# Two paddings in the SBUF layout: the activation pairs of a two-layer encoder and decoder begin 64 bytes behind a multiple of 128

## The reference

```python
for l in range(2):                                   # encoder
    h = h + 0.5 * swiglu_ffn(rms_norm(h), ffn1_w_in[l], ffn1_w_out[l])     # 1024 -> 2 x 2816 -> 1024
    h = h + hybrid_mixer(rms_norm(h), ...)           # stick-breaking heads and gated-delta heads, in and out projection
    h = h + memory_cross_attention(rms_norm(h), rms_norm(mem), ...)
    h = h + 0.5 * swiglu_ffn(rms_norm(h), ffn2_w_in[l], ffn2_w_out[l])
x = rms_norm(h)
for l in range(2):                                   # decoder
    x = hybrid_layer(x, ...)                         # three kinds of attention, gates, up and out projections
```

## Time and profile before

| | |
|---|---|
| median of 3 runs | 1866.68 us |
| the profiled execution's own time | 1862.87 us |
| its span, first to last instruction | 1861.1 us |
| TensorE busy, matmuls | 1832.1 us, 98% |
| VectorE busy | 1221.3 us, 66% |
| ScalarE busy | 961.9 us, 52% |
| DMA engines, mean | 48.5% of 16 engines' span, 162 GB/s |
| granted TensorE clock | 1.00 of full speed throughout |

### The profile page before, as it was taken

One profiled execution on the slowest core, in us unless ns is written; L12 is line 12 of the kernel. 1 busy time (PEld: TensorE's weight loads), 2 busy tenths in 40 slices (PEclk: granted clock), 3 DMA queues, 4 the chain that ended last, 5 costly groups with the idle time before them and its releaser, 6 DMA issues.

```text
span 1861.1 us, 35544 instructions
## 1 busy us (share of the span) xinstructions
PE 1832.1 (98%) x15226; PEld 1736.5 (93%) x15226; DVE 1221.3 (66%) x1876; ACT 961.9 (52%) x1475; POOL 67.9 (4%) x32
## 2 busy tenths in 40 slices
PE   7999999999999999999999999999999999999999
PEld 7999998899999999999988999999988989988889
DVE  6775576765766567756767657665774678763676
ACT  6544467364544455444673545444653565553562
POOL 0000011400000000000114000000000000000000
PEclk9999999999999999999999999999999999999999
DMA  8565543333555655555433335555446435446332
GB/s 330 194 193 183 173 145 114 103 126 124 182 189 185 205 186 188 183 187 174 148 113 102 127 114 181 187 187 182 159 158 205 136 104 179 160 147 215 125 114 91
DMA packets 84460, 302.39 MB, mean 162 GB/s; under 512 B 9168, under 2 KB 11728, under 8 KB 84176
## 3 DMA queue, kind: packets, MB, share of 16 engines
q1 hardware_dynamic: 84304, 300.13, 48.5%
HBM read 299.04 MB, written 1.05 MB: 161 GB/s over the span
## 4 chain that ended last, share of the span: by engine, by line
PE 92%; DVE 5%; ACT 2%; issue 1%; DMA 0%; SPq 0%; DVEq 0%; ACTq 0%
PE bank L395 23%; PE bank L398 22%; PE bank L399 22%; PE bank L701 2%; PE bank L930 1%; DVE w_lo L1564 1%; PE bank L417 1%; PE bank L416 1%; PE bank L413 1%; PE bank L628 1%; PE bank L1015 1%; PE bank L460 1%; PE bank L1066 1%; PE bank L464 1%; PE bank L465 1%; PE bank L903 1%
## 5 line engine op out<-in xcount | busy, mean ns | idle before, releaser
L1564 DVE TENSOR_TENSOR w_lo<-ring,w_hi 128x1024 fp32r<-128x1024 f32 x544 | 660.0, 1248 | 112.2 <-ACT w_hi L1133 111.5
L1133 ACT ACTIVATE w_hi<-ring 128x1024 fp32r<-128x1024 f32 x544 | 564.5, 1055 | 276.9 <-PE bank L395 220.8
L395 PE MATMUL bank<-xs,w_hi 128*128 128x256 f32 x2448 | 691.6, 283 | 0.0
L399 PE MATMUL bank<-xs,w_lo 128*128 128x256 f32 x2448 | 682.1, 279 | 0.0
L398 PE MATMUL bank<-xs,w_hi 128*128 128x256 f32 x2448 | 682.1, 279 | 0.0
L395 PEld LDWEIGHTS bank<-xs,w_hi 128*128 128x128 f32 x2448 | 462.8, 189 | 4.9 <-issue 3.8
L398 PEld LDWEIGHTS bank<-xs,w_hi 128*128 128x128 f32 x2448 | 460.2, 188 | 3.1 <-issue 2.9
L399 PEld LDWEIGHTS bank<-xs,w_lo 128*128 128x128 f32 x2448 | 461.2, 188 | 0.0
L398 PE MATMUL bank<-a,w_hi 128*128 128x256 f32 x704 | 199.0, 283 | 0.0
L395 PE MATMUL bank<-a,w_hi 128*128 128x256 f32 x704 | 198.7, 282 | 0.0
L399 PE MATMUL bank<-a,w_lo 128*128 128x256 f32 x704 | 197.7, 281 | 0.0
(11 more groups left out here) (393 smaller groups left out, 3048.8 us busy)
## 6 DMA issues: line engine op xcount, KB each, us to landing
ring<-in_w SPq DMA_DIRECT2D x560, 512.0 KB, 3.3
arena<-in_mem SPq DMA_DIRECT2D x2, 1024.0 KB, 12.7
const<-in_const SPq DMA_DIRECT2D x1, 1395.0 KB, 16.2
h<-in_x SPq DMA_DIRECT2D x1, 768.0 KB, 7.7
out<-h SPq DMA_DIRECT2D x3, 256.0 KB, 2.5
dec_par<-in_dec SPq DMA_DIRECT2D x1, 615.0 KB, 19.4
h<-in_x SPq DMA_DIRECT2D x1, 256.0 KB, 5.5
out<-h SPq DMA_DIRECT2D x2, 128.0 KB, 2.0
```

What stands on the lines that cost most here:

```text
L395: last = nc.tensor.matmul(o, wh, hi(x, k0 + k), start=k == 0, stop=False, skip_group_check=True)
L399: last = nc.tensor.matmul(o, wl, hi(x, k0 + k), start=False, stop=k == nk - 1, skip_group_check=True)
L1133: nc.scalar.activation(w_hi[:, s * UNIT:(s + 1) * UNIT], ring[:, u % RU, :], AF.Copy).then_inc(sems("w_hi"), 1)
L1564: nc.vector.tensor_tensor(w_lo[:, r * UNIT:(r + 1) * UNIT], ring[:, r, :], w_hi[:, s * UNIT:(s + 1) * UNIT].bitcast(F32), ALU.subtract).th ...
```

## The change

It adds a pad ahead of the arena, so that the arena begins at 64 modulo 128 (96 bytes further on); it rounds the cursor up to 32 floats, which is 128 bytes, whenever `parts` takes tiles; and it replaces an equality by a maximum, since the cursor may now stand further on. An assertion holds the four places. No instruction is added, removed or moved.

```diff
+        if (64 - here()) % 128:
+            sb("arena_pad", (64 - here()) % 128 // 4)
+        arena_at = here()
+        assert ring_at % 128 == 0 and hi_at % 128 == 0 and xs_at % 128 == 64 and arena_at % 128 == 64
         room = (nc.sbuf_bytes_remaining // 4 // 8) * 8 - 64
-        arena_at = here()
         arena = sb("arena", room)
...
         def parts(name, k):
-            n0 = at[0]
+            n0 = at[0] = -(-at[0] // 32) * 32
             return take(k, 2, T), rounded(name, k * 2 * T, arena_at + 4 * n0)
...
         obf, ob = parts("ob", 8)
-        assert at[0] == after_pairs
+        at[0] = max(at[0], after_pairs)
```

## The result

The changed kernel takes 1856.6 us (median of 6 runs, 1847.8 to 1864.2) against 1867.3 us (6 runs, 1865.3 to 1869.0): 0.994 of the time before, 95% interval 0.9923 to 0.9956, 10.7 us less. The profiled execution took 1858.5 us, with a span of 1856.8 us, 4.3 us less than the one before.

A forecast was written before the change was run, and what follows sets the result against it. TensorE's matmul-to-matmul distance was taken to bound the kernel. Gains for the moved tiles summed to 13.1 us, giving 1853.6 from the median of 1866.7, or 1855.9 with a slow first feed-forward; forecast 1854, range 1842 to 1861 us.

The forecast's parts named there:

- TensorE's distance is the time: Whole kernel: time is the sum of distances between successive matmuls; TensorE has one in flight for 98% of the span.
- Placement sorts the distances: Two-part matmuls: moving operand at 96 or 0 modulo 128 follows at 120 ns, at 64 at 113.3 or 117.8.
- Two rhythms, kept over a stage: Operands at 64 modulo 128: stable rhythms of 113.3 and 117.8 ns, each kept until something disturbs it.
- `a`: Feed-forwards: 528 matmuls in the first gain 3.5 us in the quick rhythm, 1584 in the others 3.5 in the slow.
- `ob` and `mg`: 768 matmuls behind small attention matmuls, either rhythm possible; middle gain of 4.45 ns each, 3.4 us.
- `xo`: 384 matmuls behind the attention's fp32 matmuls, taken in the slow rhythm at 2.2 ns gain each, 0.8 us.
- `ms`: Mixer: 288 of 384 matmuls gain 6.5 ns each, 1.9 us; the other pieces end before a wait on VectorE.
- `yx` at 0: Its placement modulo 128 stays at 64, so its gain was put at 0 us.
- `xs` stays as it is: `xs` and the weights stay in place, most of `xs` keeps its rhythm; any change there was put at zero.
- The median's guess: First feed-forward's `xs` may be slow in timed runs, 4.8 us; then `a` there gains 1.2 instead of 3.5 us.
- The rule against it: Documented independent TensorE read ports: placement would change nothing, 1866.7 us; the rival that placement is not the reason had 9%.

The follow-up runs named there:

- the grid: Streams of matmuls alone, no other computation, 16 pairs of placements in steps of 32 bytes modulo 128, four starts each; 113.3 to 120.1 ns per matmul.
- all64off: Changed kernel with every placement moved by 64 bytes, so M (moving operand's place less the weights', modulo 256) is 64 instead of 192; 1876.3 us, ratio 1.0041.
- again: The changed kernel once more, unchanged, for a second profile; 1856.0 us, ratio 0.9929 against the kernel before.
- w192a128: Changed kernel with weights at 192 and `xs` and the arena's pairs at 128 modulo 256; 1859.1 us, ratio 0.9946 against the kernel before.
- w32a224: Changed kernel with weights at 32 and `xs` and the arena's pairs at 224 modulo 256; 1860.3 us, ratio 0.9963 against the kernel before.
- only_a: Kernel before with, of the tiles TensorE reads in two parts, only `a` moved, to 64 modulo 128; 1862.5 us, ratio 0.9974.
- the second: Streams alone, placements in steps of 32 bytes modulo 256, 16 starts per pair; mean 115.6 to 120.0 ns with the weights at 0.

## Why the prediction was right

Forecast 1854 us in a range of 1842 to 1861; measured 1856.6. Point by point:

**TensorE's distance is the time.** Right. Nothing else changed: the waits are those of the earlier trace rows to within 1 us. In the later kernels the mean distance of each tile times its count, with 1.5 us for each fall of the clock, gives the difference of the spans from the kernel before to within 2 us, but for the two quickest: there the spans are 31.7 and 28.6 us shorter, where the sum says 35.6 and 33.8.

**Placement sorts the distances.** Right, shown by the grid with nothing else running, by `xs` moved the other way (23 us slower), and by `a` moved alone. The rule by which it was put, 64 modulo 128, was too coarse. What the runs show to count is the difference of the two places modulo 256, at steps of 32 bytes; at steps of 16 not even that decides alone. That the pad which gives 64 modulo 128 gave M = 192 for all tiles, and not 64, was luck: with M = 64 throughout (all64off) the kernel took 1876.3 us, slower than before.

**Two rhythms, kept over a stage.** Right: each start in the grids takes one of two values at M = 64 and 192, behind its first distances, and keeps it to its end. `a` took over the rhythm of `xs` in all four feed-forwards, where both have M = 192.

**The terms.** `a`: 3.5 + 3.5 us forecast, 2112 x 3.3 = 7.0 measured, with the quick feed-forward another than I thought. `ob` and `mg`: 3.4 forecast, 384 x 2.2 + 384 x 4.6 = 2.6 measured. `xo`: 0.8, measured 384 x 2.6 = 1.0. `ms`: 1.9, measured 288 x 3.4 = 1.0, since most of it fell into the slow rhythm. `yx` at 0 is the term that was wrong in kind: it stayed at 64 modulo 128, but went from M = 64 to M = 192, and gained 384 x 2.3 = 0.9 us. The sum is 12.5 against 13.1 forecast.

**`xs` stays as it is.** Wrong in mechanism, and right in size by luck. The prediction named a change of the rhythm of `xs` over whole feed-forwards as a sign of its being wrong, and that came twice: the first feed-forward turned slow (+4.7 us), the third quick (-4.7). The two cancel. The decoder's pieces fell slow more often, so `xs` cost 8000 x 0.42 = 3.4 us more in this profile, a term that the prediction had at zero. With 4.6 us for the falls of the clock, another such term, -12.5 + 3.4 + 4.6 = -4.5 us, where the spans say -4.3. So the terms are accounted for in the profiled executions. The 10.7 us between the medians are mostly those of executions without a trace, and what rhythms they had is not known.

**The median's guess**, that the first feed-forward of the timed runs may be in the slow rhythm, is not shown either way. In six profiles with `xs` at M = 192 (the kernels before, after, again, w192a128, w32a224, only_a) it was slow in four, but quick in the kernel before and in only_a. Of all 24 feed-forwards in them four were quick.

**The rule against it.** The Trainium skill, "SBUF — State Buffer", "Who interferes with whom", has TensorE's read ports for the moving operand and for the weight load independent, and nothing that TensorE waits for. Here the place of one against the other changes the distance by 6%, with no other engine at work. The Trainium skill's "TensorE: Matmul & The Clock Gate", section "Wait — 56ns, not 53.3ns?", gives columns / 2.4 GHz and 2.5 ns for matmuls back to back, an estimate of 109.2 ns for 256 columns. No stretch of this study that was averaged came under 113.2 ns. Whether the 4 ns between them are what is left of the same effect or a cost of their own, no run here tells.

What stays open: why M modulo 256 works as it does, what in a restart picks the rhythm, and why splitting `w_lo` from `w_hi` by 128 leaves only the quick one. The runs map this, and don't explain it. Nor was the full kernel run with unsplit weights at 0 and the activations at 192; for the part of the split the streams speak, with 6 of 12 quick starts against 12 of 12 there.

## What to carry to other kernels

Where TensorE runs back to back with a weight load for every matmul, count matmuls in windows: busy shares hide several per cent, and equal instructions in different stages should be equally far apart. If they aren't, compare the places of the stationary and the moving operand modulo 256 before anything else; a pad is free. Test a placement in streams alone with many different restarts, take one that is quick from every start, and put exactly that pair of places into the kernel, since neither a difference modulo 128 nor one modulo 256 carried over safely. Four starts are too few: the pair at 32 and 224 was quick from all four in the first grid, from 13 of 16 in the second, and in none of the four feed-forwards of its kernel.

## What the runs showed of the hardware that was not expected

The same matmul (128x128 by 128x256, fp32r) follows the last one after a mean of 113.3 to 120.6 ns, by the places of its operands in SBUF. At some places there are two stable rhythms, 113.3 and 117.8 ns; one holds over 1500 matmuls and a change of tensor, and can differ from one execution to the next. With the low weights 128 bytes from the high ones modulo 256, and the activations 192 from the high ones, the slow rhythm was gone from the full kernel: 1856 to 1831 us, and the spread of the runs from 16 to 1.5 us. And at the same difference of 112, weights at an odd multiple of 16 bytes took 1891 us, activations at one 1835 us.
